# Three products of rounded halves for some of the mixers' columns and gates, their low parts made by GpSimd

## The chip, the cores and the metric

The kernel runs on one core of one Trainium2 chip. The core has a matrix engine (TensorE, PE in the profile), VectorE (DVE), ScalarE (ACT), GpSimd (POOL) and SyncE (SP, which here only issues DMAs). The metric is the device time of one execution in microseconds. All engines run programs of their own and meet only at semaphores.

## The reference, cut to what matters

Everything is float32, for 256 tokens of 1024 features. Two layers of the first kind come first, then a retention layer with a dense feed-forward, then a gated convolution with a mixture of 8 experts. The change touches only the two layers of the first kind, and in them only products with `w_in`:

```python
def _layer(x, li, ...):
    xn = _rms(x, norm_mix_g)
    z = jnp.einsum('btd,dc->btc', xn, w_in)          # 1024 x 7756
    (m_qk, m_v, m_o, m_if, s_q, s_ckv, i_q, i_k, i_w, d_q, d_k, d_v, g_pre) = _split_cols(z)
    m_qk = jax.nn.silu(_causal_conv(m_qk, conv_w, conv_b))
    ...                                              # h = mlstm(...): branch 0
    ckv = _rms(s_ckv, kv_norm_g)
    kv = jnp.einsum('btr,rc->btc', ckv, w_kv_up)     # ... sparse attention by top-64 keys: branch 1
    ...                                              # differential attention: branch 2
    gates = jax.nn.sigmoid(g_pre + b_gate).reshape(B, T, 3, D_MODEL)
    merged = sum(gates[:, :, i] * (y_i @ w_branch[i]) for i in range(3))
    x = x + merged @ w_out
    g, u = jnp.split(_rms(x, norm_ffn_g) @ w_gate_up, 2, axis=-1)
    return x + (jax.nn.silu(g) * u) @ w_down
```

## The kernel before, in words

**Weights.** SyncE streams all weights in the order of their use into `ring`, six places of 128 x 2048 floats (1 MB each), called units. A unit's place is loaded anew when the semaphore recorded in `unit_read` says that it has been read. TensorE's code is written first and records these values; the code of ScalarE and VectorE then uses what it recorded.

**Two ways to multiply.** A plain product (`mm` on float32 operands, as in `chunk_tiles` and the old `feature_major`) reads the unit in the ring directly; the trace shows each such product as two instructions. The other way (`mm3`, L481) takes both operands as a high part rounded to fp32r and a low part, the rest, and sums high x high, high x low and low x high, each one instruction. The feed-forwards, the retention, the convolution, `w_out` and the experts already use it: there ScalarE makes the high part of a weight unit (`expert_high`, `half_highs`) and VectorE the low part (`weights_low`, `half_lows`), both into buffers beside the ring.

**A mixer layer on TensorE** (`layer`, from L773), all in one written order. After the norm, two calls of `feature_major` make the 1024 columns of m_qk transposed (two units each; 32 products 128 x 128 by 256). Then `columns` multiplies chunks of 440 or 512 columns, each of two units and 16 products (8 blocks of the 1024 features by 2 token tiles): ckv, index, then a wait for `kvn_dve` (L797: VectorE's normed ckv) before its transposes, then sq, the small kv product, v, index scores, o, dq, head scores, dk, dv. `gates(1)` is interleaved with the sparse attention's probabilities, then come the mLSTM weights, `branch(1)`, `mlstm_values`, `gates(0)`, the differential attention's scores (`head_scores(2)`) and `gate_tiles(2)`, which is interleaved with `turn_diff`. Each gate chunk adds a bias by one more fp32r product per token tile. Results land in eight PSUM banks, given out in turn; `hand` passes a bank to ScalarE or VectorE, and `fill` waits until it was emptied.

**Around it.** ScalarE empties the chunks (`z_evac`, L1355), copies the m_qk banks into `cpad`, applies silu to each of eight convolved tiles, and takes square roots and exponentials, all in one order. VectorE convolves (`convolve`, L1827: per tile one TENSOR_SCALAR and three SCALAR_TENSOR_TENSOR, each waiting for the one before), sums the squares of ckv and norms it, then does rotary embeddings, top keys, scores, mLSTM rows and merges. GpSimd has no work.

Of the kernel before, what the change touches and what calls it, by code (L numbers as in the profile page):

```python
# [45 lines left out]
LAYER_HALVES = DEPTH * KT  # L46
RET_HALVES = 8 * 2 + 8 * 4 + 2 * KT
# [60 lines left out]
def build(nc, a, out):  # L108

    ctx = ExitStack()  # L110
    with ctx:
# [14 lines left out]
        x = sb("x_resid", [P, TT, D])  # L126
        ring = sb("ring", [P, RING, UNIT])
# [35 lines left out]
        with ExitStack() as room:  # L163
            oT_high = room.enter_context(nc.sbuf_tensor("oT_high", [P, 2 * KT, SEQ], F32R))
        xs = sb("xs", [P, TT, D])
# [61 lines left out]
        cu = overlay("conv_u", 80 * K, [P, KT, SEQ])  # L227
        bank = [ctx.enter_context(nc.psum_tensor(f"bank{i}", [P, HALF], F32)) for i in range(8)]
# [38 lines left out]
        low_made = signal("weights_low")  # L267
        x_low = signal("inputs_low")
# [44 lines left out]
        unit_of_half, half_read, half_free = [], [], []  # L313

# [69 lines left out]
        def _(eng):  # L384
# [9 lines left out]
            half_added = [0, 0]  # L394

# [22 lines left out]
            def take_half(j, by_column):  # L418

                if j == 0:  # L420
                    issued[0] += 1
                h = n_half[0]
                n_half[0] += 1
                unit_of_half.append((issued[0] - 1, j, by_column))
                if len(half_free) <= h:
                    half_free.append(half_read[h - HALVES])
                if j == 1:
                    unit_read.append((half_low, h + 1))
                eng.wait_ge(half_low.sem, h + 1)
                return place_half(h, by_column)  # L430

# [42 lines left out]
            def read_by(sig, units):  # L474

                unit_read.extend([(sig, sig.marked)] * units)

# [171 lines left out]

            def feature_major(who, tiles=4):  # L650
# [122 lines left out]
            def layer(li):  # L773
# [3 lines left out]
                for _ in range(2):  # L777
                    feature_major("act")
                    point("qk")

                def columns(z_chunk, name=None):
                    chunk(z_chunk[1])
                    if name:
                        point(name)

                def gate_tiles(branch):
                    for i in range(2):
                        yield from chunk_tiles(512, bias=6 * li + 2 * branch + i)
# [6 lines left out]
                columns(z_ckv, "ckv")  # L795
                columns(z_index, "index")
# [3 lines left out]
                columns(z_if_sq, "sq")  # L800
# [387 lines left out]
        def _(eng):  # L1188
# [73 lines left out]

            def input_highs(gain):
# [86 lines left out]
            def layer(li):  # L1350
                norm(G_MIX + 8 * li, order=BY_TILE[2:] + BY_TILE[:2] if li else BY_TILE)
                for c in range(4):
                    copy(cpad[:, 2 * c:2 * c + 2, 3:SEQ + 3], view=lambda b: b[:, :].rearrange("p (f t) -> p f t", f=2))

# [18 lines left out]
                def exps():  # L1373

                    for j in range(6):
                        tt, ns, hs = score_bank(j)
# [7 lines left out]
                z_evac(*z_ckv)  # L1384
                for f in range(KT):
# [61 lines left out]
                last_gates((0,), 1)  # L1447
                for j in range(3):
                    copy(pT[:, j % 2, :])
                    if j == 0:  # L1450
                        last_gates((1,), 1)
# [110 lines left out]
        def _(eng):  # L1562
# [263 lines left out]

            def convolve(li):  # L1827
# [107 lines left out]
            def layer(li):  # L1935
# [3 lines left out]
                then(V.memset(v_ext[:, :, :, M_DH:M_DH + 1], 1.0))  # L1939
                convolve(li)  # L1940
# [101 lines left out]
                mlstm_weights()  # L2042
                merge(1, True)
# [211 lines left out]

        @block.sync
# [167 lines left out]
```

## Time and profile before

| | |
|---|---|
| median of 3 runs | 2644.29 us (2641.5 to 2644.31) |
| the profiled execution, its own time | 2644.26 us |
| its span, first to last instruction | 2642.5 us |
| mean granted TensorE clock | 0.995 |
| TensorE busy | 2592.0 us, 98% |
| VectorE busy | 1775.2 us, 67% |
| ScalarE busy | 1411.4 us, 53% |
| GpSimd busy | 0.2 us |

The difference between span and time, 1.8 us, lies before the first and after the last instruction. Busy times are sums of one execution. A matmul's own duration in the trace includes a tail that lies over its successor; the time that a group occupies the engine is its busy time divided by its count, or the distance between two starts.

### The profile page before, as it was taken

How to read it: one execution, taken by the hardware profiler on the slowest of the kernel's cores; microseconds unless marked ns; L12 is line 12 of the kernel's file. 1: busy time of each engine (PE TensorE's matmuls, PEld its weight loads, DVE VectorE, ACT ScalarE, POOL GpSimd, SP SyncE). 2: the span in 40 equal slices, each digit the busy share in tenths (PEclk: the TensorE clock that was granted, in tenths of full speed). 3: DMA queues.
4: the chain of work that ended last, by engine and by line, in shares of the span. 5: the costliest groups of instructions: out<-in, count | busy, mean ns of one | idle time of the engine just before them, and what ended most of it. 6: DMA issues, size and time to landing. Idle time of an engine off the chain costs nothing.

```text
span 2642.5 us, 29246 instructions
## 1 busy us (share of the span) xinstructions
PE 2592.0 (98%) x11626; PEld 1988.5 (75%) x11626; DVE 1775.2 (67%) x1953; ACT 1411.4 (53%) x1523; POOL 0.2 (0%) x4
## 2 busy tenths in 40 slices
PE   8999999999999999999999998999999999999998
PEld 5555588865555888978788897878787888888886
DVE  3754554337545444735544567999999999999997
ACT  2333344323333443354544446777777777777775
POOL 0000000000000000000000000000000000000000
PEclk9999999999999999999999998999999999999999
DMA  6343455524324554545555455989999999899995
GB/s 215 130 147 108 148 206 188 170 100 144 133 97 180 201 191 167 186 149 191 176 191 191 145 190 190 373 323 378 323 378 325 373 328 377 323 358 346 355 345 196
DMA packets 273635, 610.12 MB, mean 231 GB/s; under 512 B 10476, under 2 KB 47522, under 8 KB 273338
## 3 DMA queue, kind: packets, MB, share of 16 engines
q1 hardware_dynamic: 273466, 607.67, 64.8%
q8 instruction: 131, 2.15, 0.3%
q14 instruction: 38, 0.31, 0.0%
HBM read 606.58 MB, written 1.05 MB: 230 GB/s over the span
## 4 chain that ended last, share of the span: by engine, by line
PE 90%; DVE 5%; ACT 3%; issue 1%; DMA 0%; SPq 0%; DVEq 0%; ACTq 0%
PE bank L462 87%; DVE split L1644 3%; PE bank L707 1%; PE bank L492 1%; ACT split L1194 1%; ACT xs L1194 1%; ACT parts L1194 0%; DVE tmp L1694 0%; DVE parts L1706 0%; ACT L1194 0%; DMA pbuf<-in_gain_rows 0%; ACT pbuf L1194 0%; DVE x_resid L1679 0%; ACT ybuf L1194 0%; ACT halves L1194 0%
## 5 line engine op out<-in xcount | busy, mean ns | idle before, releaser
L462 PE MATMUL bank<-split,parts 128*128 128x512 f32 (+1 forms) x6432 | 1463.7, 388 | 3.6 <-DVE parts L1633 2.8
L462 PEld LDWEIGHTS bank<-split,parts 128*128 128x128 f32 x6432 | 1189.3, 188 | 245.6 <-issue 4.4
L1194 ACT ACTIVATE split<-ring 128x2048 fp32r<-128x2048 f32 x444 | 850.9, 1920 | 496.4 <-PE bank L462 495.7
L1644 DVE TENSOR_TENSOR split<-ring,split 128x2048 fp32r<-128x2048 f32 x444 | 993.8, 2285 | 70.7 <-ACT split L1194 70.3
L462 PE MATMUL bank<-ring,xnT 128*128 128x512 f32 (+2 forms) x896 | 367.6, 567 | 0.0
L462 PEld LDWEIGHTS bank<-ring,xnT 128*128 128x128 f32 x896 | 169.4, 190 | 180.0 <-issue 178.9
L1706 DVE TENSOR_TENSOR parts<-bank,parts 128x512 fp32r<-128x512 f32 x128 | 82.4, 686 | 157.9 <-ACT parts L1194 157.8
L1194 ACT ACTIVATE halves<-ring 128x1024 fp32r<-128x1024 f32 x96 | 101.3, 1059 | 148.3 <-PE bank L462 148.3
L1658 DVE TENSOR_TENSOR halves<-ring,halves 128x1024 fp32r<-128x1024 f32 x96 | 116.4, 1224 | 78.5 <-ACT halves L1194 78.0
L1194 ACT ACTIVATE z<-bank 128x512 f32<-128x512 f32 (+2 forms) x52 | 29.5, 568 | 234.3 <-PE bank L462 234.2
L462 PEld LDWEIGHTS bank<-xparts,halves 128*128 128x128 f32 x960 | 115.5, 192 | 3.2 <-issue 1.6
L462 PE MATMUL bank<-xparts,halves 128*128 128x256 f32 x960 | 115.9, 283 | 1.6 <-DVE xparts L1633 1.6
L1696 DVE SCALAR_TENSOR_TENSOR tmp<-bank,xsum,tmp 128x512 f32<-128x512 f32 (+1 forms) x38 | 27.5, 723 | 112.8 <-PE bank L462 112.8
L462 PE MATMUL bank<-halves,xparts 128*128 128x512 f32 x384 | 88.6, 391 | 0.0
L462 PE MATMUL bank<-ring,ybuf 128*128 128x512 f32 x192 | 84.1, 594 | 3.5 <-ACT ybuf L1194 3.5
L462 PEld LDWEIGHTS bank<-halves,xparts 128*128 128x128 f32 x384 | 71.8, 188 | 15.2 <-issue 0.5
L1194 ACT ACTIVATE parts<-bank 128x512 fp32r<-128x512 f32 x128 | 68.3, 586 | 10.7 <-PE bank L707 10.7
L1679 DVE TENSOR_TENSOR x_resid<-bank,x_resid 128x512 f32<-128x512 f32 x60 | 40.9, 690 | 48.1 <-PE bank L462 48.1
L1694 DVE TENSOR_TENSOR tmp<-bank,tmp 128x512 f32<-128x512 f32 x112 | 72.5, 683 | 0.7 <-PE bank L462 0.3
L462 PEld LDWEIGHTS bank<-ring,ybuf 128*128 128x128 f32 x192 | 35.8, 190 | 46.5 <-issue 42.1
L462 PE MATMUL bank<-split,oT_high 128*128 128x512 f32 x288 | 68.1, 393 | 0.0
L1194 ACT ACTIVATE tmp<-bank 128x512 f32<-128x512 f32 x120 | 64.6, 588 | 0.0
(259 smaller groups left out, 1748.5 us busy)
## 6 DMA issues: line engine op xcount, KB each, us to landing
ring<-in_moe_w_gate SPq DMA_DIRECT2D x112, 1024.0 KB, 7.9
ring<-in_moe_w_up SPq DMA_DIRECT2D x112, 1024.0 KB, 7.5
ring<-in_moe_w_down SPq DMA_DIRECT2D x112, 1024.0 KB, 7.5
ring<-in_w_gate_up SPq DMA_DIRECT2D x44, 1024.0 KB, 6.0
ring<-in_w_in SPq DMA_DIRECT2D x40, 1024.0 KB, 7.1
ring<-in_ret_w_in SPq DMA_DIRECT2D x24, 1024.0 KB, 5.1
ring<-in_w_down SPq DMA_DIRECT2D x22, 1024.0 KB, 6.7
ring<-in_w_in SPq DMA_DIRECT2D x20, 880.0 KB, 6.7
```

Of the source, the lines that this page charges most:

```text
L462: return nc.tensor.matmul(o, l, r, start=first, stop=final, **kw)
L492: ins = nc.tensor.transpose(bank[b][:, i * P:i * P + rows], src_of(i), ident[0:rows, 0:rows])
L707: return [nc.tensor.transpose(bank[b[tt]][:, f * P:(f + 1) * P], hb[:, tt, f * P:(f + 1) * P], ident) for f in range(n // P)]
L1194: return nc.scalar.activation(out, in_, func, **kw)
L1644: V.tensor_tensor(split[:, split_place(m), 1, :], ring[:, n % RING, :], split[:, split_place(m), 0, :].bitcast(F32), ALU.subtract).then_in ...
L1658: V.tensor_tensor(low, half_of(n, j, by_column), high.bitcast(F32), ALU.subtract).then_inc(half_low.sem, half_low.tick())
L1679: ins = V.tensor_tensor(o, b[:, :], o, ALU.add)
L1694: ins = V.tensor_tensor(hb[:, tt, 0:n], b[:, 0:n], sg[:, tt, 0:n], ALU.mult)
L1696: ins = V.scalar_tensor_tensor(hb[:, tt, 0:n], b[:, 0:n], xsum[:, 3, tt:tt + 1], sg[:, tt, 0:n], ALU.mult, ALU.mult)
L1706: V.tensor_tensor(low, b[:, 0:n].rearrange("p (f t) -> p f t", t=P), high.bitcast(F32), ALU.subtract).then_inc(hidden_low.sem, 1)
```

## The change

In each of the two mixer layers the second `feature_major`, the chunks ckv, index and sq, and the gates of branches 0 and 2 become `mm3` products: 16 units a layer (LAYER_COLUMNS). Nothing else is multiplied otherwise; `gates(1)`, v, o, dq, dk, dv and the first `feature_major` stay plain.

For each of these units ScalarE copies the ring's unit to a rounded high part (`column_highs`), in places that overlay buffers not yet used: four places for the first eight units, two in turn for the gates' units 8 to 13, one more for unit 14, and the first again for unit 15. GpSimd then subtracts the high part from the unit and writes the low part over the unit itself, in the ring (`ring_low` is the ring's memory seen as fp32r). TensorE waits for it. The inputs are split too: `mix_high` and `gate_in_high` by ScalarE, `xs_low` and `xnT_low` by VectorE. In the merging of the last gate tiles, ScalarE now empties both tiles of the last chunk after the first `pT` copy.

```diff
+        def column_place(c):
+            i = c % LAYER_COLUMNS
+            if i < 8:
+                return columns_high[i % 4]
+            return gates_high[2 if i == 14 else 0 if i == 15 else i % 2]
 ...
+            def take_column(shape):
+                n, c = issued[0], len(unit_of_column)
+                issued[0] += 1
+                i = c % LAYER_COLUMNS
+                before = {14: [], 15: [c - 3]}.get(i, [c - 4] if 4 <= i < 8 else [c - 2] if i > 9 else [])
+                column_free.append([column_read[j] for j in before] + place_free.pop(i, []))
+                ...
+                eng.wait_ge(column_low.sem, c + 1)
 ...
+            def split_chunk(n, part, bias=None):
+                b = [fill(ALL) for _ in range(TT)]
+                for u in range(2):
+                    if bias is not None and u == 0:
+                        for tt in range(TT):
+                            mm(bank[b[tt]][:, 0:n], bias_row[:, bias:bias + 1].broadcast_to([P, P]), bias_parts[:, 0:n],
+                               True, False)
+                    w = take_column((4, n))
+                    ins = []
+                    for tt in range(TT):
+                        c = slice(tt * P, (tt + 1) * P)
+                        for k in range(4 * u, 4 * u + 4):
+                            ins.append(mm3(bank[b[tt]][:, 0:n], lambda i: part(i, k)[:, c], lambda i: w[i][:, k % 4, :],
+                                           k == 0 and bias is None, k == KT - 1))
+                    if u == 0:
+                        ins[-1].then_inc(used.sem, used.tick())
+                        columns_done(used, 1)
+                    else:
+                        hand(ins[3], b[0], "act")
+                        hand(ins[7], b[1], "act")
+                        columns_done(for_act, 1)
+                    yield
 ...
-                for _ in range(2):
-                    feature_major("act")
-                    point("qk")
+                feature_major("act")
+                point("qk")
+                eng.wait_ge(mix_low_made.sem, pe.next(mix_low_made))
+                split_feature_major("act")
+                point("qk")
-                columns(z_ckv, "ckv")
-                columns(z_index, "index")
+                columns(z_ckv, "ckv", True)
+                columns(z_index, "index", True)
-                columns(z_if_sq, "sq")
+                columns(z_if_sq, "sq", True)
+                place_free[8] = place_free[9] = [(for_act, for_act.marked)]
+                eng.wait_ge(mix_low_made.sem, pe.next(mix_low_made))
                 gates(0)
                 head_scores(2)
+                place_free[14] = [(for_dve, for_dve.marked)]
 ... ScalarE
+            def column_highs(count):
+                for _ in range(count):
+                    ...
+                    eng.wait_ge(loaded[n % RING].sem, 16 * (n // RING + 1))
+                    for sig, value in column_free[c]:
+                        eng.wait_ge(sig.sem, value)
+                    A(column_place(c)[:, 0:size], ring[:, n % RING, 0:size],
+                      ACT.Copy).then_inc(column_high.sem, column_high.tick())
             def layer(li):
                 norm(...)
+                for i in range(2):
+                    A(mix_high[i][:, :, :], xnT[:, 4 * i:4 * i + 4, :], ACT.Copy).then_inc(mix_high_made.sem, mix_high_made.tick())
+                column_highs(2)
                 for c in range(4):
                     copy(cpad[...])
+                    if c in (1, 3):
+                        column_highs(2)
                 def gates(branch):
                     for i in range(2):
+                        column_highs(2)
                         z_evac(C_G + (2 * branch + i) * HALF, HALF, ACT.Sigmoid)
                 z_evac(*z_ckv)
+                column_highs(2)
                 evac_features(None, yT[:, 1, :, :], (0, 1))
+                A(gate_in_high[:, :, :], xnT[:, :, :], ACT.Copy).then_inc(mix_high_made.sem, mix_high_made.tick())
                 turned_heads(2)
+                column_highs(2)
                 roots(hsum[:, 2, kY:kY + 8], hsum[:, 1, kY:kY + 8])
                 gates(0)
-                exps()
+                exps(highs_at=3)
+                column_highs(1)
 ... VectorE: mix_lows() ahead of convolve(li); xnT_low after mlstm_weights()
+        @block.gpsimd
+        def _(eng):
+            for c, (n, size) in enumerate(unit_of_column):
+                eng.wait_ge(column_high.sem, c + 1)
+                nc.gpsimd.tensor_tensor(ring_low[:, n % RING, 0:size], ring[:, n % RING, 0:size],
+                                        column_place(c)[:, 0:size].bitcast(F32),
+                                        ALU.subtract).then_inc(column_low.sem, column_low.tick())
```

## Rows read from the trace of the kernel before

**Rows 1.** The page, busy time, share and instructions of each engine.

```profile
PE 2592.0 (98%) x11626; PEld 1988.5 (75%) x11626; DVE 1775.2 (67%) x1953; ACT 1411.4 (53%) x1523; POOL 0.2 (0%) x4
```

**Rows 2.** A stage by time: length, then busy us (count) per engine, clock, DMA share, GB/s.

```profile
47.00:71.00 24.00, 24.00 (x70) 12.48 (x69) 12.88 (x37) 10.50 (x20) 0.00 (x0) 1.00 0.47 164
```

**Rows 3.** TensorE by form: names, shapes, count, busy us, mean ns, idle before.

```profile
L462 PE MATMUL bank<-ring,xnT 128*128 128x512 f32 x512 | 224.5, 593 | 0.0
L462 PE MATMUL bank<-xparts,halves 128*128 128x256 f32 x960 | 115.9, 283 | 1.6 <-DVE xparts L1633 1.6
L462 PE MATMUL bank<-halves,xparts 128*128 128x512 f32 x384 | 88.6, 391 | 0.0
```

**Rows 4.** ScalarE in order of time, first layer: start, duration, idle before and its releaser.

```profile
26.33 0.60 ACT L1194 ACTIVATE qkbuf<-bank 128x512 f32<-128x512 f32 x1 [10.05 <-PE bank L462]
33.23 0.60 ACT L1194 ACTIVATE qkbuf<-bank 128x512 f32<-128x512 f32 x1 [6.31 <-PE bank L462]
47.05 0.60 ACT L1194 ACTIVATE qkbuf<-bank 128x512 f32<-128x512 f32 x1 [6.30 <-PE bank L462]
58.86 0.54 ACT L1194 ACTIVATE z<-bank 128x440 f32<-128x440 f32 x1 [5.37 <-PE bank L462]
60.71 2.56 ACT L1194 ACTIVATE qkbuf<-qkbuf 128x256 f32<-128x256 f32 x8
64.58 0.21 ACT L1194 ACTIVATE hsum<-hsum 128x2 f32<-128x2 f32 x1
```

**Rows 5.** The page, costliest groups: one high and one low part.

```profile
L1194 ACT ACTIVATE split<-ring 128x2048 fp32r<-128x2048 f32 x444 | 850.9, 1920 | 496.4 <-PE bank L462 495.7
L1644 DVE TENSOR_TENSOR split<-ring,split 128x2048 fp32r<-128x2048 f32 x444 | 993.8, 2285 | 70.7 <-ACT split L1194 70.3
L1194 ACT ACTIVATE halves<-ring 128x1024 fp32r<-128x1024 f32 x96 | 101.3, 1059 | 148.3 <-PE bank L462 148.3
L1658 DVE TENSOR_TENSOR halves<-ring,halves 128x1024 fp32r<-128x1024 f32 x96 | 116.4, 1224 | 78.5 <-ACT halves L1194 78.0
```

**Rows 6.** VectorE in order of time, first layer's start to its normed ckv.

```profile
11.38 0.75 DVE L1621 TENSOR_SCALAR xs<-x_resid,xsum 128x1024 f32<-128x1024 f32 x1
33.94 0.41 DVE L1833 TENSOR_SCALAR qkbuf<-qkbuf,gcol 128x256 f32<-128x256 f32 x1 [16.45 <-ACT qkbuf L1194]
34.39 1.53 DVE L1836 SCALAR_TENSOR_TENSOR qkbuf<-qkbuf,gcol 128x256 f32<-128x256 f32 x3
47.68 0.41 DVE L1833 TENSOR_SCALAR qkbuf<-qkbuf,gcol 128x256 f32<-128x256 f32 x1 [6.10 <-ACT qkbuf L1194]
59.43 0.43 DVE L1746 TENSOR_TENSOR tmp<-z 128x256 f32<-128x256 f32 x1 [4.12 <-ACT z L1194]
65.02 0.62 DVE L1967 TENSOR_SCALAR yb<-z,hsum 128x256 f32<-128x256 f32 x2
```

**Rows 7.** TensorE in order of time: first product, ckv's transposes, gates(0), gates(2).

```profile
17.27 29.74 PE L462 MATMUL bank<-xnT,ring 128*128 128x256 f32 x128 [1.02 <-ACT xnT L1194]
...
70.47 0.60 PE L492 MATMUL bank<-const,yb 128*128 128x128 f32 x4
...
223.65 0.48 PE L462 MATMUL bank<-bias_parts,bias_row 128*128 128x512 f32 x1
...
252.14 1.04 PE L492 MATMUL bank<-const,yb 128*128 128x128 f32 x8
...
256.47 0.50 PE L462 MATMUL bank<-bias_parts,bias_row 128*128 128x512 f32 x1
...
285.40 0.60 PE L492 MATMUL bank<-const,pbuf 128*128 128x128 f32 x4
```

**Rows 8.** VectorE's slowest instruction per element, and the scores and weights beside gates(2).

```profile
145.91 0.68 DVE L1820 TENSOR_TENSOR_SCAN ybuf<-ybuf 4x256 f32<-4x256 f32 x1
...
254.30 0.69 DVE L1930 SCALAR_TENSOR_TENSOR pbuf<-bank,const 128x512 f32<-128x512 f32 x1 [20.32 <-PE bank L462]
...
265.39 0.25 DVE L2048 RECIPROCAL psum_row<-psum_row 128x16 f32<-128x16 f32 x1 [1.23 <-ACT pbuf L1194]
```

More of the change, by code:

```diff
@@ L126, in build @@
         x = sb("x_resid", [P, TT, D])
+        with ExitStack() as room:
+            ring_low = room.enter_context(nc.sbuf_tensor("ring_low", [P, RING, UNIT], F32R))
         ring = sb("ring", [P, RING, UNIT])
@@ L164, in build @@
             oT_high = room.enter_context(nc.sbuf_tensor("oT_high", [P, 2 * KT, SEQ], F32R))
+            xs_low = oT_high[:, 0:KT, :]
+            xnT_low = oT_high[:, KT:2 * KT, :]
         xs = sb("xs", [P, TT, D])
@@ L227, in build @@
         cu = overlay("conv_u", 80 * K, [P, KT, SEQ])
+        at_tile = 4 * ZW
+        at_gates = 4 * (C_G - C_O)
+        at_heads = 4 * (ZF + TT * M_HEADS * (M_DH + 1))
+        at_pbuf = at_heads + 4 * (CP + KT * SEQ)
+        columns_high = [overlay("columns_high0", at_gates, [P, UNIT], F32R),
+                        overlay("columns_high1", at_tile + at_gates, [P, UNIT], F32R),
+                        overlay("columns_high2", at_pbuf + 4 * 3 * HALF, [P, UNIT], F32R), ybuf_tmp_high[:, 0:UNIT]]
+        mix_high = [overlay(f"mix_high{i}", i * at_tile + at_gates + 4 * UNIT, [P, KT // 2, SEQ], F32R) for i in range(TT)]
+        gates_high = [overlay("gates_high0", 4 * (C_IF - C_O), [P, UNIT], F32R),
+                      overlay("gates_high1", at_tile + 4 * (C_IF - C_O), [P, UNIT], F32R),
+                      overlay("gates_high2", at_heads + 4 * UNIT, [P, UNIT], F32R)]
+        gate_in_high = overlay("gate_in_high", at_heads, [P, KT, SEQ], F32R)
         bank = [ctx.enter_context(nc.psum_tensor(f"bank{i}", [P, HALF], F32)) for i in range(8)]
@@ L430, in take_half @@
                 return place_half(h, by_column)
+            def take_column(shape):
[4 more added lines that the diff above has]
+                column_free.append([column_read[j] for j in before] + place_free.pop(i, []))
+                k, width = shape
+                unit_of_column.append((n, k * width))
+                eng.wait_ge(column_low.sem, c + 1)
+                whole = (column_place(c)[:, 0:k * width], ring_low[:, n % RING, 0:k * width])
+                return [v.rearrange("p (k c) -> p k c", k=k) for v in whole]
             def half_done(ins=None, sig=None):
@@ L648, in chunk, with mix_part, gate_part, split_feature_major @@
                     pass
+            def mix_part(i, k):
+                return xs_low[:, k, :] if i else mix_high[k // 4][:, k % 4, :]
+            def gate_part(i, k):
+                return xnT_low[:, k, :] if i else gate_in_high[:, k, :]
+            def split_chunk(n, part, bias=None):
[20 more added lines that the diff above has]
+                    yield
+            def split_feature_major(who):
+                w = [take_column((4, 512)) for _ in range(2)]
+                for fp in range(2):
+                    b = fill(ALL)
+                    for f in range(2):
+                        for k in range(KT):
+                            c = (2 * fp + f) * P
+                            ins = mm3(bank[b][:, f * SEQ:(f + 1) * SEQ], lambda i: w[k // 4][i][:, k % 4, c:c + P],
+                                      lambda i: mix_part(i, k), k == 0, k == KT - 1)
+                    hand(ins, b, who)
+                columns_done(for_act, 2)
             def feature_major(who, tiles=4):
@@ L775, in layer, with columns @@
                 xnT_wait()
-                for _ in range(2):
-                    feature_major("act")
-                    point("qk")
-                def columns(z_chunk, name=None):
-                    chunk(z_chunk[1])
+                feature_major("act")
[3 more added lines that the diff above has]
+                point("qk")
+                def columns(z_chunk, name=None, split=False):
+                    if split:
+                        for _ in split_chunk(z_chunk[1], mix_part):
+                            pass
+                    else:
+                        chunk(z_chunk[1])
                     if name:
@@ L787, in gate_tiles @@
                     for i in range(2):
-                        yield from chunk_tiles(512, bias=6 * li + 2 * branch + i)
+                        b = 6 * li + 2 * branch + i
+                        yield from (chunk_tiles(512, bias=b) if branch == 1 else split_chunk(512, gate_part, bias=b))
                     point("gates")
@@ L1825, in mlstm_scans, with mix_lows @@
                 eng.wait_ge(row_dve.sem, dve.latest(row_dve))
+            def mix_lows():
+                for i in range(2):
+                    eng.wait_ge(mix_high_made.sem, dve.next(mix_high_made))
+                    ins = V.tensor_tensor(xs_low[:, 4 * i:4 * i + 4, :], xnT[:, 4 * i:4 * i + 4, :],
+                                          mix_high[i][:, :, :].bitcast(F32), ALU.subtract)
+                ins.then_inc(mix_low_made.sem, mix_low_made.tick())
             def convolve(li):
@@ L1939, in layer @@
                 then(V.memset(v_ext[:, :, :, M_DH:M_DH + 1], 1.0))
+                mix_lows()
                 convolve(li)
@@ L2042, in layer @@
                 mlstm_weights()
+                eng.wait_ge(mix_high_made.sem, dve.next(mix_high_made))
+                ins = V.tensor_tensor(xnT_low, xnT[:, :, :], gate_in_high[:, :, :].bitcast(F32), ALU.subtract)
+                ins.then_inc(mix_low_made.sem, mix_low_made.tick())
                 merge(1, True)
```

23 lines of the change are left out of this document (20 added, 3 removed).

## The prediction

> **What bounds the kernel now.** I read the page's busy shares first: TensorE is busy for 2592.0 of 2642.5 us and GpSimd idle [rows 1]. Then the stages: between 47 and 71 us TensorE is busy for all of 24.00 us at full granted clock, and VectorE for 12.88 [rows 2]. Then each engine in order of time through the first mixer layer: TensorE never idles there for more than a microsecond, and ScalarE empties banks at TensorE's beat, 6.9 us apart, idle 6.3 us before each [rows 4]. So the mixers are bound by TensorE, and a cheaper product is worth its whole difference until a producer is late. The second layer repeats the first 520 us later, so I work one out and double it.
>
> **What the products save.** A plain 512-column product is two instructions (512 for 256 products) [rows 3]. With its bias, a token tile of gates takes (252.14 - 223.65) / 4 = 7.12 us [rows 7]. An fp32r instruction of 512 columns occupies TensorE for 88.6 / 384 = 0.231 us, one of 256 columns for 115.9 / 960 = 0.121 us [rows 3]. For 440 columns I put 0.200 us between them.
> - Second m_qk call: 47.05 - 33.23 = 13.8 us [rows 4]; new 32 x 3 x 0.121 = 11.6. Saves 2.2.
> - A chunk of 440: 58.86 - 47.05 = 11.8 us [rows 4]; new 16 x 3 x 0.200 = 9.6. Saves 2.2, three times 6.6.
> - A gate chunk: 2 x 7.12 = 14.2 us; new 48 x 0.231 for products and 2 x 0.231 for the biases = 11.5. Saves 2.7, four times 10.8.
>
> Together 19.6 us a layer, 39.2 us in all, if nothing is late. The splitting decides how much of it stays.
>
> **The price of one unit.** ScalarE's high part takes 1.92 us for 2048 and 1.06 for 1024 [rows 5], so 1.7 for the 1760 of a narrow unit. The low part, a two-operand subtraction, has no row on GpSimd. On VectorE it takes 2.29 us [rows 5]: the low end. The dearest rate per element in this trace is the scan's, 0.68 us for 256 [rows 8]; carried to 2048 elements in full it is 5.4 us, the high end. Without its fixed part (about 0.16 us) the scan costs 0.52 / 256 = 2.03 ns an element, 4.2 us for 2048 and 3.6 for 1760. I take that, since GpSimd does here in software what VectorE streams. The Trainium skill, "GPSIMD Engine Reference", section "Performance versus the Vector engine", gives 4497 ns for this very shape and 2293 for VectorE (this trace: 2285); with it the sum below would be 2641.
>
> **What of it lies beside other work.** ScalarE's 16 highs, two `mix_high` of 1.06 and one `gate_in_high` of 1.92 are some 33 us a layer in its idle times; VectorE's two `mix_lows` of 1.22 fall into its 16.45 us wait before the convolution [rows 5, 6], and `xnT_low`, 2.3 us, into its wait before branch(1)'s first bank. The first two units: inputs are there at 17.3 [rows 7], highs at 21.3 and 23.2, lows at 25.5 and 29.7; TensorE wants both at 33.1. Cover 3.4 us, less by about 1.7 in the second layer. At 5.4 us a unit they still arrive in time. SyncE gets no new wait, and the first unit of each chunk is released half a chunk earlier; a reload takes 7 us and has more. ScalarE's reordered emptying of the last gate tile costs nothing: eight banks are in turn.
>
> **The wait for ckv's norm.** TensorE reaches it after m_qk, ckv and index, so 6.6 us earlier than 70.47 [rows 7]: at 63.9. Behind it on TensorE stands everything. Its chain: ckv's last bank now at 54.4; ScalarE empties it (54.95), then makes two highs (58.3) ahead of a table load, silus and root, which took from 59.4 to 64.8 [rows 4]; so root at 63.7, and VectorE's 0.9 us [rows 6] make it 64.5. Without any hindrance to VectorE TensorE waits 0.6 us.
>
> **VectorE beside GpSimd.** No row shows the two together, so both ends: GpSimd costs VectorE nothing, or excludes it for each whole instruction. Rows lean to the second. One-operand work from SBUF runs at 0.75 us for 1024 elements [rows 6], two-operand work takes 1.22 [rows 5]: VectorE has two streams in, and a second operand uses up what doubled the one-operand rate. GpSimd, with two operands from SBUF, must get at one of them. I take full exclusion for instructions with two SBUF operands and for the doubled ones, each side getting its turn after the other's instruction. The Trainium skill, "SBUF — State Buffer", section "Who interferes with whom", says just this: the shared port pair is an exclusive lock held for a whole instruction. By it the sum is the one below; were it wrong, the first rival's.
>
> The convolution is 8 tiles of one one-operand and three two-operand steps, 1.9 us each [rows 6]. Half of it starts at 33.9, half after 45.4. GpSimd's units 2 to 7 run at 35.9, 40.0, 47.1, 51.2, 56.6 and 60.7, 3.6 us each, and VectorE gets one step between two that follow each other closely. By my count it is done at 69.5 instead of 53.1, the sums at 71.4, the norm at 72.5. TensorE waits 8.6 us at 63.9 and goes on 2.1 us later than before. The sq chunk takes back 2.2. What follows (rope, key norms, top keys) has over 10 us of slack and no GpSimd beside it. Net so far: 0.
>
> **The gates.** Two places in turn: unit 10's high can't start before TensorE has read unit 8, and ScalarE is held by a root until 231.1. A unit with biases takes 24 x 0.231 + 0.46 = 6.0 us, one without 5.5. On the old clock: unit 8 runs 223.6 to 229.5, 9 to 235.05; unit 10's high is there at 233.0, its low at 237.2: TensorE waits 2.2. Unit 11 is ready before 243, then 12 and 13 behind turned heads and scores are in time, until 264.4. Unit 14's high waits for VectorE's last score bank. The scores start 2.2 us after gates(0) ends, as before (254.30 against 252.14) [rows 7, 8], at 250.9, and the sixth bank is read 8.9 us later; in between, unit 13's subtraction (until 254.8) holds a tiny one-operand step of the first bank for 2.6 us. So 262.4, high 264.3, low 268.5: TensorE waits 4.1 at 264.4. VectorE's weights, at 265.39 before [rows 8], now wait for units 14 and 15 on GpSimd; `turn_diff` comes at 275.6 and TensorE waits 1.2. It ends unit 15 at 281.5 instead of 285.4 [rows 7]. Net: 3.9 of 10.8 us stay.
>
> **Sum.** 0.1 + 3.9 = 4.0 us a layer, 8 us in all. Against the profiled execution's 2644.26 us, which stands 0.03 below the median of 2644.29, that is **2636 us**.
>
> **Rivals.**
> 1. *GpSimd doesn't hinder VectorE.* For it: nothing in this trace; against it: the two streams above. Then TensorE waits 0.6 us at ckv's norm, 2.2 at unit 10 and 1.5 at unit 14 (score banks done 2.6 earlier), so 19.6 - 4.3 = 15.3 us a layer stay (by my clocks 15.8), 31 us in all: 2613 us; with lows of 2.3 us 2608.
> 2. *Slower than before: the subtraction is dear and excludes VectorE.* Place: the convolution before ckv's norm, and unit 14. Six subtractions stand in the convolution's way, so each microsecond of price puts off the norm by about 6 and unit 14 by 3. At the high end, 5.4 us (4.65 narrow), the norm comes at 78.8 (TensorE 6 us later than before behind sq) and the gates save nothing: 6 us lost a layer, 2656. It decides from about 4.7 us a unit. For it: a software engine has no row here; against it: it needs the scan's full rate.
> 3. *Half a hindrance*: the engines share, VectorE at half rate. The norm is late by about 5 us, unit 14 by 3: some 10 us a layer stay, 2624.
> 4. *The change doesn't do what it says*: a matmul of these operands runs at another rate. The fp32r rows have the same shapes and loads; I leave it 2 in 100.
>
> **Chances.** Forecast 0.48 (2628 to 2648), first rival 0.24 (2606 to 2619), second 0.17 (2649 to 2664), third 0.09, fourth 0.02. A measurement tells 0.2%, 5.3 us, from no change. Faster than 2639: rivals 1 and 3 and somewhat over half of the forecast, 0.59. Within: the rest of the forecast, 0.22. Slower: 0.19. The range, for 8 in 10, is 2609 to 2653: both unknown ends less their tails. The forecast's own is 2628 to 2648.
>
> **What would show it.** Right: plain `ring,xnT` products of 512 columns halve in count and GpSimd shows 32 TENSOR_TENSOR of about 4.2 and 3.6 us; VectorE's SCALAR_TENSOR_TENSOR on `qkbuf` have a mean far above 0.49 us, or gaps, only beside GpSimd; TensorE waits some 8 us before `yb`'s transposes, 2 us at unit 10, 4 at unit 14, in both layers. Wrong: those steps keep their 0.49 us (rival 1), a subtraction over 4.7 us (rival 2), TensorE waiting for units 2 to 7 themselves, or long gaps after the ckv stage, where I count on slack.

## The result and the profile after

The changed kernel takes 2650.06 us in the median of nine runs (2648.1 to 2654.05); the kernel before took 2643.91 beside it (2641.3 to 2644.68). The ratio is 1.0025, 95% interval 1.0015 to 1.0035: slower by 0.25%. I had forecast 2636, so the direction is wrong; the time lies inside the range of 2609 to 2653 and above the forecast's own, 2628 to 2648. The profiled execution took 2654.05 us (span 2652.3), the slowest of the nine, with a mean granted clock of 0.987 where the kernel before had 0.995.

The page, busy time per engine, answers to [rows 1]. TensorE has 25 us less to do, and GpSimd is busy for 141 us:

```profile
PE 2566.9 (97%) x11914; PEld 2037.4 (77%) x11914; DVE 1859.0 (70%) x1959; ACT 1475.0 (56%) x1561; POOL 141.3 (5%) x36
```

GpSimd by form (names, shapes, count; busy us, mean ns; idle before): its price, for which [rows 5] had only VectorE's and ScalarE's. The first row is the gates, half of all units.

```profile
L2405 POOL TENSOR_TENSOR ring_low<-ring,gates_high 128x2048 fp32r<-128x2048 f32 x16 | 74.4, 4660 | 359.5 <-ACT gates_high L1299 359.5
L2405 POOL TENSOR_TENSOR ring_low<-ring,columns_high 128x1760 fp32r<-128x1760 f32 x8 | 32.5, 4071 | 16.4 <-ACT columns_high L1299 16.4
L2405 POOL TENSOR_TENSOR ring_low<-ring,columns_high 128x2048 fp32r<-128x2048 f32 x4 | 18.0, 4519 | 288.7 <-ACT columns_high L1299 288.7
```

VectorE by form between 30 and 75 us: the convolution's steps, 0.41 and about 0.49 us each in [rows 6].

```profile
L1975 DVE SCALAR_TENSOR_TENSOR qkbuf<-qkbuf,gcol 128x256 f32<-128x256 f32 x24 | 26.1, 1088 | 0.9
L1972 DVE TENSOR_SCALAR qkbuf<-qkbuf,gcol 128x256 f32<-128x256 f32 x8 | 10.7, 1334 | 12.9 <-ACT qkbuf L1299 12.9
```

In order of time (start, duration) one sees which steps they are. First VectorE, then GpSimd:

```profile
35.35 4.09 DVE L1972 TENSOR_SCALAR qkbuf<-qkbuf,gcol 128x256 f32<-128x256 f32 x1
39.48 5.14 DVE L1975 SCALAR_TENSOR_TENSOR qkbuf<-qkbuf,gcol 128x256 f32<-128x256 f32 x3
...
56.09 8.77 DVE L1975 SCALAR_TENSOR_TENSOR qkbuf<-qkbuf,gcol 128x256 f32<-128x256 f32 x3
...
256.75 0.69 DVE L2070 TENSOR_REDUCE nmax<-pbuf 128x4 f32<-128x512 f32 x1
257.48 3.23 DVE L2071 TENSOR_SCALAR nmax<-nmax 128x4 f32<-128x4 f32 x1
...
267.14 4.51 DVE L2071 TENSOR_SCALAR nmax<-nmax 128x2 f32<-128x2 f32 x1
...
276.59 4.49 DVE L2202 SCALAR_TENSOR_TENSOR pbuf<-pbuf,psum_row,tmp 128x128 f32<-128x128 f32 x1
```

```profile
35.07 4.23 POOL L2405 TENSOR_TENSOR ring_low<-ring,columns_high 128x1760 fp32r<-128x1760 f32 x1 [3.64 <-ACT columns_high L1299]
39.26 4.04 POOL L2405 TENSOR_TENSOR ring_low<-ring,ybuf_tmp_high 128x1760 fp32r<-128x1760 f32 x1
```

A step of 0.41 us that starts beside GpSimd ends when GpSimd's instruction does: 35.35 to 39.44, GpSimd 35.07 to 39.30. The last row of VectorE is the third weight difference of the first `turn_diff`, 0.35 us in the kernel before. The small steps ahead of it, 0.17 us alone, last 3.23 and 4.51 us and end with GpSimd's subtractions at 256.12 to 260.69 and 267.03 to 271.62. The reduction of an SBUF tile at 256.75 runs beside the first of these and keeps the 0.69 us that it takes alone.

TensorE's waits (us in total, times, longest), those new with the change:

```profile
PE bank L543 <- DVE yb L2107: 20.5, 2, 10.3
PE bank L543 <- DVE pbuf L2202: 8.4, 2, 4.2
PE bank L507 <- POOL ring_low L2405: 5.4, 4, 2.0
```

And TensorE in order of time at the places of [rows 7]:

```profile
73.56 1.11 PE L543 MATMUL bank<-const,yb 128*128 128x128 f32 x4 [10.22 <-DVE yb L2107]
85.92 4.46 PE L507 MATMUL bank<-ring,ckvT 128*128 128x512 f32 x10
...
226.85 0.71 PE L507 MATMUL bank<-bias_parts,bias_row 128*128 128x512 f32 x2
...
253.87 1.03 PE L543 MATMUL bank<-const,yb 128*128 128x128 f32 x8
...
281.72 1.12 PE L543 MATMUL bank<-const,pbuf 128*128 128x128 f32 x4 [4.21 <-DVE pbuf L2202]
```

What the waits don't tell stands in the windows around the first one (length; busy us and count of PE, PEld, DVE, ACT, POOL; granted clock; DMA share; GB/s):

```profile
64.00:68.00 4.00, 0.00 (x0) 0.00 (x0) 3.79 (x9) 0.83 (x2) 0.06 (x1) 1.00 0.80 262
68.00:72.00 4.00, 0.00 (x0) 0.00 (x0) 3.75 (x10) 1.85 (x3) 0.00 (x0) 0.53 0.01 2
72.00:76.00 4.00, 2.44 (x9) 2.29 (x10) 3.00 (x12) 2.18 (x5) 0.00 (x0) 0.50 0.00 2
76.00:80.00 4.00, 4.00 (x16) 3.67 (x15) 2.93 (x13) 1.90 (x4) 0.00 (x0) 0.69 0.00 0
80.00:84.00 4.00, 4.00 (x22) 3.74 (x21) 3.62 (x16) 0.29 (x1) 0.00 (x0) 1.00 0.36 96
```

TensorE stops at 63.3; about five microseconds later the clock falls to 0.50 (1.2 GHz for 2.4), and it is back only five microseconds after TensorE has gone on at 73.56. The sq chunk runs in that time: from its transposes to kv's first product 12.36 us, where the kernel before took 12.26 with dearer products. The saved 2.2 us are gone.

The second mixer layer, stage by stage (us between the starts of TensorE's rows; the first layer's own first stage varies by 2 us between executions, so I take the second). The last three columns are experiments told below.

| stage | before | after | eleven products | all three waits filled | low parts on VectorE, tile moved |
|---|---|---|---|---|---|
| first product to ckv's transposes | 51.33 | 54.85 | 54.84 | 54.87 | 45.03 |
| to kv's first product (sq) | 12.25 | 12.62 | 10.11 | 10.11 | 10.10 |
| to gates(0) | 140.93 | 140.94 | 144.70 | 140.92 | 141.02 |
| to `turn_branch` (gates(0)) | 28.48 | 26.95 | 25.37 | 25.39 | 23.82 |
| to gates(2) | 4.34 | 4.75 | 4.75 | 4.74 | 4.74 |
| to the first `turn_diff` | 21.39 | 23.08 | 23.08 | 23.09 | 17.62 |
| to its product with the values | 7.98 | 8.94 | 8.70 | 6.48 | 6.44 |
| sum | 266.70 | 272.13 | 271.55 | 265.60 | 248.77 |

### The profile page after: what moved, and what is told of

It is laid out like the page before. It is cut to its first block, busy times and chain, and to the rows that moved or that the text cites. A ratio compares the mean times of both kernels' runs of the same rounds, so it can differ in the third digit from the quotient of the medians.

```text
span 2652.3 us, 29926 instructions
## 1 busy us (share of the span) xinstructions
PE 2566.9 (97%) x11914; PEld 2037.4 (77%) x11914; DVE 1859.0 (70%) x1959; ACT 1475.0 (56%) x1561; POOL 141.3 (5%) x36
## 3 DMA queue, kind: packets, MB, share of 16 engines
HBM read 606.58 MB, written 1.05 MB: 229 GB/s over the span
## 4 chain that ended last, share of the span: by engine, by line
PE 84%; DVE 11%; ACT 3%; issue 1%; POOL 0%; DMA 0%; SPq 0%; DVEq 0%; ACTq 0%
PE bank L507 81%; DVE split L1776 3%; DVE qkbuf L1975 2%; PE bank L802 1%; PE bank L543 1%; ACT split L1299 1%; DVE qkbuf L1972 1%; DVE nmax L2071 1%; ACT parts L1299 0%; ACT xs L1299 0%; DVE pbuf L2202 0%; DVE tmp L1826 0%; DVE parts L1838 0%; POOL ring_low L2405 0%; DVE pbuf L2069 0%
## 5 line engine op out<-in xcount | busy, mean ns | idle before, releaser
L507 PE MATMUL bank<-ring,xnT 128*128 128x512 f32 (+2 forms) x448 | 183.6, 567 | 0.0
L507 PEld LDWEIGHTS bank<-ring,xnT 128*128 128x128 f32 x448 | 84.5, 190 | 90.3 <-issue 89.9
L2405 POOL TENSOR_TENSOR ring_low<-ring,gates_high 128x2048 fp32r<-128x2048 f32 x16 | 74.4, 4660 | 359.5 <-ACT gates_high L1299 359.5
```

What stands on the lines that cost most here:

```text
L507: return nc.tensor.matmul(o, l, r, start=first, stop=final, **kw)
L2405: nc.gpsimd.tensor_tensor(ring_low[:, n % RING, 0:size], ring[:, n % RING, 0:size], column_place(c)[:, 0:size].bitcast(F32), ALU.subtract) ...
```

## The experiments

My theory after the result: GpSimd holds VectorE for each whole instruction, that makes TensorE wait, and each wait is paid a second time in granted clock. A ratio compares a kernel with the kernel before as it ran beside it (medians 2642.61, 2642.64 and 2642.43 us).

### Does the clock cost, apart from the wait?

**Eleven products ahead of the wait.**

```diff
+                filler(11, ALL)      # mm(bank, ident, const[:, 0:HALF]) x 11
                 eng.wait_ge(kvn_dve.sem, pe.next(kvn_dve))
```

> The changed kernel, with eleven plain products of the identity (128x128 by 128x512, 0.86 us each, 9.5 us in all) that TensorE runs just before its wait for ckv's norm, a wait of 10.22 us in the changed kernel. Nothing that TensorE or another engine waits for changes. Theory (the waits cost twice, once as idle time and once more because the granted clock falls from 1.00 to 0.50 in them and stays there for some microseconds of the products behind them): the granted clock stays at 1.00 through 63 to 80 us, the sq chunk (12.36 us in the changed kernel) takes about 10.1, and the kernel is 2.3 us a layer faster than the changed one: about 2645.5 us, ratio to the kernel before 1.0006. Rival A (the lower clock in these microseconds is not caused by the idle time, or what it costs is hidden): 2650 us, ratio 1.0025. Rival B (the added products hold banks or the queue and push the chain behind them): 2651 to 2654.

Measured: 2650.01 us (2647.46 to 2652.05), ratio 1.0028 [1.0019, 1.0037]. By the median rival A holds. In the trace the first layer does what the theory says (TensorE in order of time):

```profile
62.02 9.60 PE L507 MATMUL bank<-const 128*128 128x512 f32 x22
71.66 0.66 PE L543 MATMUL bank<-const,yb 128*128 128x128 f32 x4
81.76 7.03 PE L507 MATMUL bank<-ring,ckvT 128*128 128x512 f32 x16
```

From transposes to kv 10.10 us for 12.36, and 10.11 for 12.62 in the second layer. But there another stage became 3.8 us longer (the table's third row). Windows of this kernel in it:

```profile
720.00:724.00 4.00, 4.00 (x18) 2.75 (x18) 2.48 (x7) 1.56 (x5) 0.00 (x0) 0.82 0.75 278
724.00:728.00 4.00, 4.00 (x9) 2.30 (x10) 1.87 (x5) 1.27 (x4) 0.00 (x0) 0.50 0.01 1
728.00:732.00 4.00, 4.00 (x18) 3.82 (x18) 0.95 (x3) 2.40 (x7) 0.00 (x0) 0.50 0.00 0
```

TensorE is busy in all of it, but with small products (64 columns, then 4 rows by 256 columns, 128x256), and the clock falls all the same. One profile can't say that this happened in the other runs too; their mean clock (0.990 or 0.991 in nine of eleven) suggests it.

**All three waits filled.** As before it, with `filler(2, ALL)` ahead of unit 10 and `filler(4, ALL)` ahead of `turn_diff(*steps[0])`.

> As the last one, and two such products ahead of TensorE's wait for unit 10 (1.86 us in the changed kernel) and four ahead of its wait for the difference of the probabilities (4.21 us). Theory (waits plus clock): the clock's share in the three places is 2.3, 2.06 and 2.9 us a layer, 14.6 us in the kernel; with all of it back 2650 - 14.6 = 2635.5 us, ratio 0.9968, a gain over the kernel before that is left when the waits themselves stand. Rival A: no effect, 2650. Rival B: the products in the gates run over the end of their waits, which are short (each can add up to its own length where the wait is over): 2640 to 2648.

Measured: 2640.97 us, ratio 0.9998 [0.9989, 1.0007]; eight runs from 2638.7 to 2641.3, three from 2646.5 to 2649.7. By the two ratios 7 us came of 14.6, in the eight lower runs 9. I had taken 14.6 from the profile of after, the dearest of its nine; in the second layer the three places give 2.51 + 1.56 + 2.46 = 6.5 us (table), and the second of them isn't lost in every execution. The waits stand; only the clock is back: in the profiled execution it stays at 1.00 through both mixer layers. Rival B gives this time too, but the trace shows 0.16 us of waiting left behind the two added products and 0.80 behind the four, so they don't run over.

**The moved tile.** To take the small products' loss away I moved one gate tile, 16 products of 512 columns, in between them (ScalarE's emptying of it moves along):

```diff
-                    if j < 4:
-                        next(between, None)
+                    if j < 2:
+                        next(between)
...
                     point("weights")
+                    if h == 0:
+                        next(between)
+                        next(between, None)
```

> The changed kernel with eleven plain products ahead of the wait for ckv's norm, and with the moved tile. The eleven products alone left the median where it was (2650.0), though in its trace the sq chunk took 10.10 us for 12.36: its small products lost the clock in the second layer (26.98 us for 23.22), and 9 of its 11 runs had a granted clock of 0.990 or 0.991. Theory (the gain of 4.6 us is real and was lost again at the small products by the run's new timing): with both, 2650 - 4.6 = 2645.5, ratio 1.0010, the clock 0.993 or more in nearly all runs. Rival (the eleven products bring nothing): 2650, as that kernel and the one with the moved tile alone.

> The changed kernel with the one tile of gates(1) moved between the mLSTM weights, as in the last study's fastest kernel; nothing else. In the changed kernel's trace the small products do not lose the clock (23.22 us in both layers), so the theory that the moved tile is worth only what it prevents expects no change: 2650 us, ratio 1.0025, 2648 to 2651. Rival (the moved tile is a gain of its own, some 2 us of waits a layer, which would also explain the 5.7 us that it brought the kernel with VectorE's low parts where 3.8 were expected): 2645 to 2647.

> The changed kernel with plain products ahead of its three long waits (eleven, two and four), and with the moved tile. Without the tile: 2641.0 us, eight runs at 2638.7 to 2641.3 with a clock of 0.995 or 0.996, three at 2646.5 to 2649.7 with 0.992 or 0.993. Theory: the three were the small products' loss; all runs now lie at 2638 to 2642 with a clock of 0.995 or more, median 2639.5, ratio 0.9988. Rival (the three were something else): as before, some at 2646 or more.

Measured: eleven products with the tile 2646.07 us (2645.46 to 2648.05), ratio 1.0012 [1.0003, 1.0021], clock 0.992 or 0.993 in all runs, the stage at 141.0 us in both layers; the tile alone 2652.73 (six runs, 2647.82 to 2655.38), ratio 1.0034 [1.0022, 1.0046], above the 2648 to 2651 that I expected. So the eleven products are worth 3.4 us (against the changed kernel, by the ratios) to 5.8 us (against the tile alone) once the small products keep the clock, and the tile alone gains nothing. With all waits filled and the tile: 2641.77 us (2638.64 to 2644.64), clock 0.995 or more in every run. The three high runs are gone as expected, the median isn't lower; that part of the expectation failed.

### Who holds whom, and at what price?

**GpSimd copies one tensor.**

```diff
-  tensor_tensor(ring_low, ring, high, ALU.subtract)
+  tensor_copy(ring_low, ring)
```

> The changed kernel with GpSimd's subtraction of two tensors replaced by its copy of one (ring_low<-ring, same sizes, places and waits; so the third products take the whole weight in place of its low part). It asks which work of GpSimd holds VectorE. If any instruction of GpSimd on these tiles does: each copy that meets the convolution stretches one of its steps to about the copy's own length, and the wait for ckv's norm stays at several us. If only one that reads two tensors does: the convolution's steps last 0.41 and 0.48 us throughout, the wait for ckv's norm is under 1 us, and the kernel takes about 2615 us.

Measured: 2604.7 us, a single run. TensorE waits 0.4 us for ckv's norm. GpSimd and a step of VectorE beside it:

```profile
L2405 POOL CAST ring_low<-ring 128x1760 fp32r<-128x1760 f32 x12 | 21.2, 1793 | 42.9 <-ACT columns_high L1299 42.9
```

```profile
33.79 1.75 DVE L1972 TENSOR_SCALAR qkbuf<-qkbuf,gcol 128x256 f32<-128x256 f32 x1
```

The expectation tied two things together that aren't: a copy does hold VectorE (0.41 us became 1.75), but it lasts 1.79 us for 4.07. Four steps of the convolution are held for 1.3 us each, and the step behind its sums for 0.9 (1.05 us); that fits the slack.

**The copy made as long as the subtraction.**

```diff
+  tensor_copy(low, ring); tensor_copy(low[half]); tensor_copy(low)   # one after the other
```

> The kernel with GpSimd's copy of one tensor (2604.7 us), each copy followed by half a copy and a whole one (in place, one after the other), so that GpSimd takes about 4.5 us for a unit as with the subtraction, but in pieces of 1.8, 0.9 and 1.8 us, none of which reads two tensors. The third products take the whole weight in place of the low part, as there. It parts GpSimd's price from what it does to VectorE. Theory (GpSimd holds VectorE during any of its instructions on these tiles, and it is the price that makes that dear): the convolution's steps stretch by 4 to 4.5 us for a unit, the wait for ckv's norm is 6 to 10 us and the kernel takes 2635 to 2650 us. Rival (a copy holds VectorE for a moment only, about 1.3 us, however many follow; it is the subtraction's second source that makes the difference): the wait is under 3 us and the kernel takes 2605 to 2618 us.

Measured: 2639.58 us, a single run. Back are TensorE's wait and VectorE's long steps:

```profile
PE bank L544 <- DVE yb L2108: 13.9, 2, 7.4
```

```profile
35.53 4.67 DVE L1976 SCALAR_TENSOR_TENSOR qkbuf<-qkbuf,gcol 128x256 f32<-128x256 f32 x3
...
52.60 4.84 DVE L1976 SCALAR_TENSOR_TENSOR qkbuf<-qkbuf,gcol 128x256 f32<-128x256 f32 x3
```

The copies differ from the other kernel's in number alone, and cost 35 us. In the second layer 8.9 of 16.7 us lie ahead of kv's first product, where TensorE waits for VectorE; in the gates TensorE waits for GpSimd's low part itself as well (2.66 and 2.75 us at unit 10 in the two layers). So it is GpSimd's time, directly and by its hold on VectorE, and it doesn't take a subtraction.

**VectorE subtracts itself.**

```diff
-        @block.gpsimd   ...   tensor_tensor(ring_low, ring, high, ALU.subtract)
+            def column_lows(count):      # VectorE, the same subtraction
+   mix_lows(); column_lows(2)            # and after tiles 0, 1, 4, 5 of the convolution,
+   column_lows(2); z_inverse(24, 25)     # in the merge, ahead of and in the scores, in the differences
```

> The changed kernel with the low parts of the sixteen units made by VectorE instead of GpSimd (2 to 2.3 us each by the 1.18 us of a 128x1024 subtraction in the trace; two before the convolution, one after each of its tiles 0, 1, 4 and 5, two while it waits for the root of ckv's norm, two in the merge, three ahead of the scores, one inside them, one behind them, one in the differences). GpSimd does nothing. Theory (the changed kernel loses by GpSimd holding VectorE, and by the clock behind the waits): VectorE's work of 32 us a layer more fits its idle stretches, the convolution's steps are back at 0.48 us, the wait for ckv's norm falls from 10.22 to about 0.7 us, those in the gates to under 1 us together, the clock stays at 1.00, and some 15 to 18 of the 19.6 us of shorter products a layer are left: 2608 to 2616 us, ratio 0.988. Rival A (what cost the time is the extra work of ScalarE, four highs ahead of the silu and the root, and the dependencies by unit, whoever subtracts): the waits stay above 5 us a layer, 2625 to 2645. Rival B (VectorE is the bound once it has 32 us a layer more): 2640 or more.

Measured: 2612.4 us (four runs, 2610.64 to 2614.05), ratio 0.9884 [0.9869, 0.9899]. VectorE by form, 14 to 75 us:

```profile
L1987 DVE SCALAR_TENSOR_TENSOR qkbuf<-qkbuf,gcol 128x256 f32<-128x256 f32 x24 | 11.6, 485 | 0.9
L1967 DVE TENSOR_TENSOR ring_low<-ring,columns_high 128x1760 fp32r<-128x1760 f32 x4 | 7.9, 1984 | 0.0
```

It pays 1.98 us for what GpSimd does in 4.07 while holding it. Both rivals are out: ScalarE's extra work is all still there, and the time is far below rival B's 2640. In the first layer the small products lose the clock again; with the tile moved they don't:

> The kernel with the low parts on VectorE (2612.4 us), with one tile of gates(1), 16 products of 512 columns, moved from between the probabilities' small products to behind the first pair of the mLSTM weights (for TensorE, and ScalarE's evacuation with it). In all runs of that kernel the mean granted clock was 0.993, and its trace has the clock at 0.50 from 190 to 200 us, where TensorE is never idle but runs small products (64 columns, and 4 rows by 256 columns), so that this stretch took 26.98 us where the others took 23.22. Theory (the clock falls on stretches of small products as it falls on waits, and which of them it meets depends on when they come): with seven microseconds of wide products in the middle the stretch stays at 1.00 in both layers, 3.8 us less, 2608.5 us. Rival A (the fall is set off by something else at that moment): 2612. Rival B (the moved tile makes the small products wait for VectorE and ScalarE that it had hidden, or the other way round): 2613 or more.

Measured: 2606.67 us (four runs, 2604.51 to 2610.66), ratio 0.9865 [0.985, 0.988]: the fastest kernel here that computes the whole result. Not all of the 5.7 us is the tile's: of the 7.2 us between the two profiled executions 3.7 lie in this stage of the first layer, and 3.3 behind the second mixer, where the clock was at 0.50 for 13.7 us instead of 20.5. Windows, first of the one without, then of the one with the tile; the small products of the mLSTM weights stand at 188 to 196 in the one, at 180 to 184 and 192 to 196 in the other:

```profile
188.00:192.00 4.00, 4.00 (x13) 2.51 (x13) 2.13 (x7) 1.64 (x5) 0.00 (x0) 0.71 0.50 180
192.00:196.00 4.00, 4.00 (x12) 2.77 (x12) 1.74 (x6) 1.60 (x4) 0.00 (x0) 0.50 0.00 0
```

```profile
180.00:184.00 4.00, 4.00 (x13) 2.14 (x13) 1.63 (x5) 2.29 (x4) 0.00 (x0) 1.00 0.00 0
...
192.00:196.00 4.00, 3.50 (x29) 3.21 (x28) 2.04 (x6) 2.34 (x8) 0.00 (x0) 1.00 0.95 362
```

**GpSimd where VectorE has slack.** The last kernel, with units 0, 1, 8 and 9 of each layer given back to GpSimd.

> The kernel with the low parts on VectorE and the moved tile (2606.7 us), but GpSimd makes those of units 0, 1, 8 and 9: the first two while VectorE waits for m_qk's banks, the others while it waits between the four banks of branch(1)'s merge. Its price of 4.5 us a unit and its hold on VectorE are as in the changed kernel. Theory (they cost where VectorE's next step is one that TensorE waits for, and nothing where it has slack): no change, 2606 to 2609. Rival (any work of GpSimd costs its own length): 4 units of 4.5 us in two layers, less 2.3 us each that VectorE no longer does, 18 us at the most: 2615 to 2625.

Measured: 2610.58 us (four runs, 2609.22 to 2610.73), ratio 0.9874 [0.9859, 0.9889], 3.9 above its neighbour, with intervals that overlap, and between the two expectations. The trace doesn't put that into the mixers: from the first product to the last stage of the table the second layer takes 248.8 us in both. In the profiled runs 2.0 of the 6.1 us lie in the first 16 us of the first layer, and 3.4 in the stages behind the second mixer, where the clock fell for longer. I can't say whether these belong to the change. It also shows which steps are free of the hold; VectorE, then GpSimd beside it:

```profile
209.74 0.69 DVE L2198 TENSOR_TENSOR xs<-bank,z 128x512 f32<-128x512 f32 x1 [2.74 <-PE bank L507]
```

```profile
204.70 9.12 POOL L2440 TENSOR_TENSOR ring_low<-ring,gates_high 128x2048 fp32r<-128x2048 f32 x2 [173.48 <-ACT gates_high L1302]
```

A product of a PSUM bank and an SBUF tile keeps its 0.69 us.

### Where the loss is

**Columns alone, gates alone.** The other part as plain products, without its high and low parts.

> The changed kernel with gates(0) and gates(2) as plain products, as before: only m_qk's second product and the ckv, index and sq chunks are split (8 units a layer on GpSimd, not 16). Theory (waits plus clock, place by place): by the trace of the changed kernel the stretch from the layer's first product to kv's first is 3.2 and 3.9 us longer than before in the two layers, 8.8 us of saved products included, and the gates add nothing: 2642.6 + 7 = 2649.5, at the most 1 or 2 us lower where the profiled run was slower than the median. Rival (the gates are where the loss is, and the columns gain): below 2642.

> The changed kernel with m_qk, ckv, index and sq as plain products, as before: only gates(0) and gates(2) are split. Theory: from gates(0) to the next layer the changed kernel took 316.94 us where the kernel before took 315.53, so 1.4 us a layer are lost there, 10.8 of saved products included: 2645.5, and where the clock falls at other moments 2643 to 2648. Rival (the columns are where the loss is, and the gates gain as predicted, 3.9 us a layer): 2635.

Measured: columns alone 2650.1 us (2648.61 to 2651.51), ratio 1.0026 [1.0017, 1.0035]; gates alone 2641.0 (2638.16 to 2644.05), ratio 0.999 [0.9981, 0.9999]. Waits of the first, then of the second kernel:

```profile
PE bank L543 <- DVE yb L2103: 19.6, 2, 10.3
```

```profile
PE bank L543 <- DVE pbuf L2191: 8.4, 2, 4.2
PE bank L507 <- POOL ring_low L2394: 5.4, 4, 2.0
```

The two differences, +7.5 and -1.6, add up to the changed kernel's +6.2 within the measurement. The gates did a little better than I expected from the profile, and gain 0.1%. Their waits are those of the changed kernel, but in the profiled execution the clock fell only at `turn_diff`, and for 3.4 us instead of 6.8: gates(0) took 25.46 and 25.39 us (27.02 and 26.95 in the changed kernel), the last stage 8.06 in both layers (8.76 and 8.94). The columns lose it all. With the kernel of VectorE's low parts the same products are a gain in both places.

## Why the prediction was wrong

Right were the products, the hold of GpSimd on VectorE and the four places where TensorE waits. By the second layer of the kernel without waits (248.77) the products save 17.9 us, and with the 0.4 for ckv's norm and 0.3 and 0.1 elsewhere 18.7, where I had 19.6. The price, 4.07 us for a narrow unit and 4.52 for a wide one (4.66 in the gates), is above my 3.6 and 4.2 and below my high end. The Trainium skill, "GPSIMD Engine Reference", section "Performance versus the Vector engine", gives 4497 ns; the trace agrees (4519). VectorE is excluded for each whole instruction, as forecast; the convolution ended at 70.4 (69.5 forecast), ckv's norm came at 73.5 (72.5).

**The step that failed** is "The sq chunk takes back 2.2" with "Net so far: 0", and its like in the gates, "Net: 3.9 of 10.8 us stay": they take the products behind a wait at full clock. The first of them ran at half. In the second layer of the profiled execution that costs 2.51 us at sq, 1.56 at unit 10 and 2.46 at `turn_diff` (after against the kernel with all waits filled), 6.5 us a layer, 13 in all.

The waits are a smaller miss. Forecast 8.6, 2.2, 4.1 and 1.2, together 16.1; measured in the second layer 10.25, 1.98, 0.73 and 4.22, and 0.34 for `ybuf`: 17.5. At ckv's norm the longer price counts six times. At unit 14 I had VectorE's score banks holding up its high, which it doesn't wait for (it waits for TensorE's scores). The hold came out at `turn_diff` instead: unit 14's subtraction stops a step of the scores for 4.51 us, which puts off the weights and unit 15's high, and unit 15's subtraction then stops a 0.35 us step for 4.49.

The sum also has a slip: 19.6 less its own waits of 16.1 leaves 3.5 us a layer, not 4.0, because in the gates 10.8 less 7.5 is 3.3 and not 3.9. Redone with what was measured, 18.7 less 17.5 leaves 1.2 us a layer: 2642 us, and the kernel with all waits filled took 2640.97. Less 6.5 for the clock it is -5.3 us a layer; measured -5.4 in the second layer and -4.8 in the first. That is the profiled execution, at 2654.05. The median is 4 us lower and its mean clock 0.989 for 0.987, so by this sum the clock cost about 8 us in most executions and not 13; the ratios of the filled kernel say 7 to 9. By either number the clock turns what would be even, or 2 us of gain, into a loss.

Rival 1 is refuted by the long steps. Rival 2 gave the right sign, and its range of 2649 to 2664 holds the time, but from the wrong term. Its price of 5.4 us was not met: 4.07 narrow and 4.66 wide stand at its threshold (4.7 wide, 4.0 narrow by its own scale), where its sum is even, and the 6 us come from the clock. Rival 3 is refuted (held, not slowed), rival 4 by 18.7 us of savings.

By my rule, which held the doubled steps and those with two SBUF operands, the convolution's one-operand step was free, since 0.41 us for 256 elements isn't the doubled rate. It is held like the others: 4.09 us. So are steps on 4 and 2 elements whose only other operand is the constant -1 (3.23 and 4.51 us for 0.17; I had forecast 2.6 for the first). The Trainium skill, "SBUF — State Buffer", section "Who interferes with whom", lets one SBUF source contend only in the doubled modes; here the measurement decides, unless these steps run in such a mode without the gain. No run parts the two.

## What to carry over

Before work goes to an idle engine, price what that engine holds up: a subtraction of 4.07 us on GpSimd stretched a step of VectorE from 0.41 to 4.1 us, and doing it itself took VectorE 1.98. Price a wait of the bounding TensorE twice, as idle time and as products at half clock behind it (here 17.5 and 6.5 us a layer in the profiled execution, and 4 rather than 6.5 in the median one). When a saving shows in its stage and not in the total, compare the other stages before calling it nothing: here a fall of the clock moved into another stage.

## What the runs showed that I had not expected

- The clock falls on busy stretches too, if the products are small: 26.98 us for 23.22 from the first product on `ybuf` of the mLSTM weights to the first on `v_ext`, in the first layer of the kernel with VectorE's low parts, with TensorE busy in every microsecond. It differs between layers and kernels with the same small products, and I have not shown what decides; seven microseconds of wide products in the middle kept it at 1.00 there in all five profiles taken with the moved tile (the stage at 141.0 us in all ten layers).
- Waits of 1.86 and 1.98 us at unit 10 brought the clock down in the changed kernel (27.02 and 26.95 us for the stage); a wait of 1.87 in the second layer of the kernel with eleven products didn't (25.37).
- GpSimd copies 1760 columns in 1.79 us, faster than VectorE subtracts them (1.98), and takes 4.07 for the subtraction.
- What the hold leaves alone, in the rows here: a reduction of one SBUF tile, and products with one operand in PSUM.
